# Landing key and value cache pages on 32 partitions instead of 128 in a paged differential attention

## What is computed

```python
k_past = cache_k[l][page_table].reshape(n_dec, -1, N_HEADS_A, 2, DK)   # 8 x 8192 x 4 heads x 2 maps x 64
v_past = cache_v[l][page_table].reshape(n_dec, -1, N_HEADS_A, DV)      # 8 x 8192 x 4 heads x 128

def diff_attn_sample(q, k_new, v_new, k_past, v_past, lam):
    s_past = einsum('bqhmd,bkhmd->bhmqk', q, k_past) * scale
    ...
    p = softmax(concatenate([s_past, s_new], axis=-1), axis=-1)
    a = p[:, :, 0] - lam * p[:, :, 1]
    return (einsum('bhqk,bkhe->bqhe', a[..., :n_past], v_past)
            + einsum('bhqk,bkhe->bqhe', a[..., n_past:], v_new))
```

## Time and profile before

| | |
|---|---|
| median of 3 runs | 3382.82 us (3381.3 to 3390.33) |
| the profiled execution: its own time | 3376.92 us |
| its span, first to last instruction | 3375.3 us |
| mean granted TensorE clock | 0.936 |
| PE busy over the span | 87% |
| DVE / ACT / POOL busy | 41% / 29% / 13% |
| read from HBM / written | 604.22 MB / 80.90 MB |
| key pages, issued by SP | 512 DMAs of 256 KB, 4.3 us from issue to landing (median) |
| value pages, issued by POOL | 512 DMAs of 256 KB, 4.5 us (median) |

### The profile page before, as it was taken

How to read it: one execution, slowest core, us unless ns; L and a number is a source line. 1 busy time by engine, 2 the same in 40 slices (tenths; PEclk the granted TensorE clock), 3 DMA queues, 4 the chain that set the end, 5 groups by cost and what they waited for, 6 DMA issues and landing times. The chain is left out here.

```text
span 3375.3 us, 55103 instructions
## 1 busy us (share of the span) xinstructions
PE 2929.0 (87%) x17753; PEld 1488.9 (44%) x17753; DVE 1373.1 (41%) x2709; ACT 973.0 (29%) x2213; POOL 442.8 (13%) x780
## 2 busy tenths in 40 slices
PE   5799999997888999999998799837999999999940
PEld 1244444444565666666666355422333333333310
DVE  2222223332677778888887345460000000000019
ACT  0122222222555666666665011100111111111114
POOL 0000000000333232222221000000000000000015
PEclk8899999998999999999999899958999999999975
DMA  9510111113998997786765644208999676755659
GB/s 346 168 37 37 37 37 37 43 38 121 356 330 306 307 311 255 247 271 217 241 210 169 189 169 162 90 8 315 329 327 349 212 271 214 252 195 197 209 198 342
DMA packets 278800, 687.69 MB, mean 204 GB/s; under 512 B 29134, under 2 KB 30414, under 8 KB 278470
## 3 DMA queue, kind: packets, MB, share of 16 engines
q1 hardware_dynamic: 208414, 455.13, 40.1%
q0 software_dynamic: 64656, 219.07, 18.1%
q10 hardware_dynamic: 5528, 11.02, 0.9%
HBM read 604.22 MB, written 80.90 MB: 203 GB/s over the span
## 5 line engine op out<-in xcount | busy, mean ns | idle before, releaser
L419 PE MATMUL z<-w_in_sb,hT 128*128 128x512 f32 (+1 forms) x1360 | 602.2, 602 | 0.7 <-ACT hT L454 0.7
L419 PEld LDWEIGHTS z<-w_in_sb,hT 128*128 128x128 f32 (+1 forms) x1360 | 255.0, 190 | 323.9 <-issue 321.6
L832 POOL DMA_DIRECT2D v_ring<-cache_v x512 | 277.0, 541 | 764.1 <-issue 759.6
L909 PE MATMUL ps_turned<-ident,k_ring 128*128 128x128 f32 x2048 | 303.7, 287 | 13.0 <-DVE kTs L1106 13.0
L1865 PE MATMUL e_gu<-wg,xT 128*64 128x512 f32 x1312 | 297.5, 607 | 15.0 <-DMA wg<-w_exp_gate 14.9
L1893 PE MATMUL e_y<-wd,ehT 128*64 128x512 f32 x1312 | 292.4, 598 | 15.2 <-DMA wd<-w_exp_down 15.2
L909 PEld LDWEIGHTS ps_turned<-ident,k_ring 128*128 128x128 f32 x2048 | 229.2, 145 | 166.9 <-issue 141.4
L1007 ACT ACTIVATE kTs<-ps_turned 128x512 f32<-128x512 f32 x384 | 224.6, 598 | 237.8 <-PE ps_turned L909 234.5
L1865 PE MATMUL e_gu<-wu,xT 128*64 128x512 f32 x1312 | 288.6, 592 | 2.1 <-DMA wu<-w_exp_up 2.1
L1936 DVE TENSOR_TENSOR hh<-e_gu,sg 128x512 f32<-128x512 f32 x41 | 28.4, 692 | 578.7 <-PE e_gu L1865 578.7
L1033 ACT ACTIVATE p_probs<-p_scores,neg_chunk_max 128x512 f32<-128x512 f32 (+3 forms) x320 | 196.5, 624 | 47.0 <-DVE neg_chunk_max L1150 46.9
(11 more groups left out here) (309 smaller groups left out, 3334.4 us busy)
## 6 DMA issues: line engine op xcount, KB each, us to landing
v_ring<-cache_v POOLq DMA_DIRECT2D x512, 256.0 KB, 4.5
k_ring<-cache_k SPq DMA_DIRECT2D x512, 256.0 KB, 4.3
wg<-w_exp_gate SPq DMA_DIRECT2D x33, 2048.0 KB, 9.4
wu<-w_exp_up SPq DMA_DIRECT2D x33, 2048.0 KB, 11.0
wd<-w_exp_down SPq DMA_DIRECT2D x33, 2048.0 KB, 9.2
scratch_y<-y SPq DMA_DIRECT2D x41, 512.0 KB, 9.2
kT<-w_ada SPq DMA_DIRECT2D x6, 2048.0 KB, 16.4
V<-w_ada SPq DMA_DIRECT2D x6, 2048.0 KB, 17.0
```

The source lines that it names most:

```text
L419: last = pe.matmul(z[0:R, c, :], hT[:, k, 0:R], w[:, k, c * 512:(c + 1) * 512], start=(k == 0), stop=(k == KD - 1))
L832: eng.dma_start(ring[:, u, j, :], cache[0, ds(page, 1)].rearrange(layout)).then_inc(arrived[u], 16)
L909: last = pe.transpose(turned("turn_k", n, h)[:, j * P:(j + 1) * P], k_ring[:, n % K_RING, j, h * P:(h + 1) * P], ident[:])
```

## The change

The destination of a page's DMA is changed, and the view of its source to match. Before, token `p` of page `j` went to partition `p`, slot `j`: 128 pieces of 2 KB, one in each partition. After, page `j` goes to partitions `32 j` to `32 j + 31`, and each of these takes four neighbouring tokens, one per slot: 32 pieces of 8 KB. The four pages of a step fill the same buffer as before. Slot `t` now holds, for all 128 partitions, the tokens `4 r + t` of each page, so that the order of the 512 keys of a step changes, for keys and values alike. The number of DMAs, their bytes, the queues that issue them and all instructions of the other engines stay as they are.

```diff
         def pages(eng, cache, layout, ring, n, u, arrived):
             for j in range(PS):
                 page = eng.value_load(table[0:1, ds(n * PS + j, 1)], min_val=0, max_val=cache.shape[1] - 1)
-                eng.dma_start(ring[:, u, j, :], cache[0, ds(page, 1)].rearrange(layout)).then_inc(arrived[u], 16)
+                rows = slice(PAGE // PS * j, PAGE // PS * (j + 1))
+                eng.dma_start(ring[rows, u], cache[0, ds(page, 1)].rearrange(layout, t=PS)).then_inc(arrived[u], 16)
...
                 def load_k(n):
                     if n >= K_RING:
                         wait_turned(sp, "turn_k", n - K_RING, H - 1)
-                    pages(sp, io["cache_k"], "o p h m d -> p (o h m d)", k_ring, n, n % K_RING, k_in)
+                    pages(sp, io["cache_k"], "o (p t) h m d -> p (o t) (h m d)", k_ring, n, n % K_RING, k_in)
...
                 def load_v(n, u, round_):
                     waited(pool, pv_done, n - V_RING + 1)
-                    pages(pool, io["cache_v"], "o p h e -> p (o h e)", v_ring, n, u, v_in)
+                    pages(pool, io["cache_v"], "o (p t) h e -> p (o t) (h e)", v_ring, n, u, v_in)
```

## The result

The changed kernel takes 3578.91 us (median of 4 runs, 3570.46 to 3582.2) against 3382.06 us: a ratio of 1.0575, 95% interval 1.0559 to 1.0591, or 197 us more. It lies within the range, 65 us above the predicted time, and on rival A (3580 us). The profiled execution took 3581.02 us with a span of 3579.4 us.

A forecast was written before the change was run, and what follows sets the result against it. Early attention steps were taken to wait for value pages, later ones for PE and its softmax partners. At 8.8 us of DMA a step, 73 + 52 + 12 + 0 gave +137 us on 3376.9, 3514 us; range 3365 to 3600.

The forecast's parts named there:

- rival A: Attention stage: no overlap at all, every page at 220 GB/s, 9.5 us a step, 203 us more, 3580 us; chance 0.24.
- the round trip of the value ring: First stretch: a buffer comes free with one step's products; the load for two steps later must issue and land meanwhile.
- Fewer, longer pieces: Page loads: 8 KB pieces could cut a step's data time about 8%, at most 16 us; counted as nothing if port-bound.
- rival C: Attention page loads: long pieces win, data time falls 8%, 5 to 25 us off, middle 3365 us; chance 0.12.
- Issuing: POOL's and SP's page DMAs: same count and look-ups, no gain counted; bounds none and 25 us over the first stretch.
- Fewer partitions per transfer: Page loads: 220 GB/s alone, 290 for a quarter of the time, mean 238 GB/s, 8.8 us a step, 137 us more.
- the zero of the last group: Last stretch, 31 steps: 9.68 us a step is longer than 8.8 us of data, so 0 us added.
- The four terms: Losses in the attention stage's four stretches of 31, 32, 32 and 31 steps: 73, 52, 12 and 0 us.
- 7 us to spare: Last stretch: values used 12.3 us after issue, landing 4 to 5 us; the spare time was to cover later landings.
- the forecast's neighbourhood: Attention steps of 8 to 9.2 us each, around the forecast's 8.8; chance 0.42.
- B: Value loads: only the landing grows, 1 us more per waiting step, 31 us in the first stretch, 3410 us; chance 0.13.
- D: Whole kernel: nothing changes, gains and losses cancel or SP's and POOL's look-ups set the pace, 3377 us; chance 0.09.

## Why the prediction was right

**What bounds the kernel before**: the prediction read the wait for values from the earlier trace rows and left two causes side by side, the bytes and the round trip of the value ring. The experiments don't part them fully. Leaving out a quarter of the bytes gives 16 us, but it takes value loads out of the round trip too. Issuing values sooner moves the wait to the prompt's queries, which speaks for the bytes. Yet with pages on every fourth partition the engines were busy 0.90 of the first stretch, not 0.95, and the time stayed. The loss itself is another matter: in the change the share is 0.99 to 1.01 in the first three stretches, and there the data set the step.

**Fewer, longer pieces**: taken as nothing for a crowded transfer. That is not borne out as it stands, since 2 KB pieces in the same place took 30 us more than 8 KB ones; the cause of these is open. As an opportunity (rival C) it was wrong too: with full reach, 8 KB pieces give 333 GB/s in the first stretch, where 2 KB pieces gave 338, and no time. The 405 GB/s of the earlier trace rows came from loads of one queue in another stretch and was no promise for this one.

**Issuing**: no gain, right. POOL's part fell from 537 to 489 ns and SP's from 333 to 316, with no effect.

**Fewer partitions per transfer**: the term that decides, and right in kind. The store over 64 partitions in the earlier trace rows gave 220 GB/s; the pages went at 235 in the first stretch, and 216 with the values in the other order. The Trainium skill ("SBUF — State Buffer", section on the DMA port swizzle) has partitions 0 to 31 and 0 to 63 reach the same 8 of 16 ports, and the other half the other 8: this case agrees, with 3579 and 3554 us for 32 and 64 neighbours, 3573 for every second of a half, and 3384 for every fourth of all. The same page of the Trainium skill ("Can I just issue two DMAs to hit both halves?") says that two DMAs on opposite halves gain some 6% over one and serialize: the 2 to 5% measured here are as small, but they compare opposite halves with the same half, two DMAs each time, and no run here has the page's comparison.

**The terms of the sum that were mis-sized** are the rate and the bytes of a step, and the zero of the last group. The rate was taken as "0.75 x 220 + 0.25 x 290 = 238 GB/s". Between the products of steps 4 and 31 it was 232, so the product came out near, but by luck: both queues had pages in flight 98% of the time (850 to 1300 us) and not half of it, the oldest lay on opposite halves 66% of the time and not 25%, and that went with 5% more and not 32%. The bytes were short: between the same two starts a step moved 2.16 MB, not 2.10, as the prompt's queries and outputs use the same engines. The earlier trace rows had shown it, 67.25 MB in the two queues for 31 steps. 2.16 MB at 232 GB/s are 9.3 us; the forecast had 8.8, and about half of the difference is bytes and half rate. The second and third group are alike (2.18 and 2.16 MB at 232 and 230 GB/s). The four terms then read 89, 69, 30 and 9 us against 73, 52, 12 and 0.

The last group isn't free, though its data alone don't set it: 2.04 MB a step at the 232 GB/s of the first would be 8.8 us, and its steps went from 9.5 to 9.8. The "7 us to spare" did not cover the landings throughout. These had a median of 9.4 us there (4.0 before), and PE waited 4.2 us in three places for values, where it waited for none before; the other half of the 9 us was not traced.

**The rivals.** A had the time (3580) by 9.5 us a step at 220 GB/s, and the measured 9.3 to 9.4 us lie nearer to it than to the forecast's neighbourhood of 8 to 9.2. Its working was off too, by a higher rate and more bytes that nearly cancel. B fell with the GB/s. C and D fell with the landings.

**What was said to show it** was there: landings over 7 us (10.0), about 240 GB/s at a DMA share of nine tenths (235 at 0.99), steps of equal length in three quarters (9.3 to 9.4 us and not 8.8). Two signs did not come. PE had no idle time before L909 (L910 now) in 850 to 1050 us: the values stayed the late ones. And POOL's 537 ns became 489.

## To carry to other kernels

Before a transfer is reshaped for longer pieces, ask which partitions it lands on: a tile within partitions 0 to 63 or 64 to 127 moved at 216 to 236 GB/s here when keys and values both landed so, and pages of the same bytes spread over every second or fourth partition of all 128 at 337 and 333 GB/s in the same place of the program. If pages must keep long pieces, interleave them over the partitions instead of stacking them. And look at the other streams of the same moment: one badly placed stream slowed a well-placed one from 22.3 to 16.0 bytes per ns and engine.

## What was not expected

- Half of the change costs nearly all of it: keys alone 88%, values alone 75% of the loss, because the badly placed stream goes with a slower other one.
- The order in which a step's value pages are issued is worth 56 us once the placing is bad (3635 against 3579 us); which halves meet explains at most a part of it.
- Pieces of 8, 4 and 2 KB in steady streams over all partitions give the same time within 0.1% (3383.9, 3382.3 and 3384 us).
- With PE idle 62 of 200 us, its granted clock averaged 0.82 in the first stretch, after 0.96, and a group of products behind a wait of 5.71 us took 1.93 us where it took 1.08, with the granted clock at 0.50, the lower of the two levels of 1.2 and 2.4 GHz. What this adds to the time was not separated; PE had time to spare there.
- With a destination of every fourth partition, SP's own time per DMA was 481 ns, where the change had 316.
